# Gate rows through DRAM instead of TensorE transposes, in a two-block transformer kernel

## The reference, cut to what matters

```
mod = (silu_c @ w_mod[l] + b_mod[l]).reshape(B, 3 * N_SUB, 1, D)
x = macaron_half_ffn(x, norm_g[l, 0], *mod_terms(mod, 0), ffn_w_in[l, 0], ffn_w_out[l, 0])
# macaron_half_ffn: x + 0.5 * gate * swiglu(modulate(x, g, shift, scale), w_in, w_out)
sh, sc, gt = mod_terms(mod, 1)
h = modulate(x, norm_g[l, 1], sh, sc)
x = x + gt * y            # y: attention and mLSTM mixer in layer 0, spatial gating in layer 1
```

## Time and profile before

| | |
|---|---|
| median of 3 runs | 1588.73 us (1588.63 to 1588.76) |
| the profiled execution, first to last instruction (span) | 1587.4 us |
| what lies around the span, against the median | 1.3 us |
| PE / DVE / ACT / POOL busy | 1565.0 / 1173.0 / 777.5 / 70.5 us |
| transposes of gate columns, first and last start | 72, at 138.1 and 1520.7 us |
| DMA, mean over the span | 212 GB/s |

### The profile page before, as it was taken

The page is one execution under the profiler, slowest core; times in us unless marked ns, Lnnn a source line. Parts: engine busy times, 40 slices in busy tenths (PEclk is TensorE's granted clock), DMA queues, the critical chain, the costliest instruction groups (busy, mean ns, idle before and its releaser), DMA issues.

```text
span 1587.4 us, 20744 instructions
## 1 busy us (share of the span) xinstructions
PE 1565.0 (99%) x7994; PEld 1296.9 (82%) x7994; DVE 1173.0 (74%) x1917; ACT 777.5 (49%) x1246; POOL 70.5 (4%) x112
## 2 busy tenths in 40 slices
PE   7999999999999999999999999999999999999998
PEld 5887778888888888887777888888888888888887
DVE  7889899759886665477766888868877667666654
ACT  5767666532222222254556555445555463455552
POOL 2000000100000000030010100000000100010000
PEclk9999999999999999999999999999999999999999
DMA  9977676336656655252122777867777575455550
GB/s 376 373 290 273 234 251 224 107 127 231 213 212 239 224 212 179 87 175 80 67 95 72 281 302 292 311 219 264 255 280 274 210 308 187 171 203 187 186 190 30
DMA packets 93044, 336.97 MB, mean 212 GB/s; under 512 B 10625, under 2 KB 11265, under 8 KB 92690
## 3 DMA queue, kind: packets, MB, share of 16 engines
q1 hardware_dynamic: 90706, 327.58, 57.0%
q0 software_dynamic: 2240, 8.06, 1.5%
HBM read 334.56 MB, written 1.05 MB: 211 GB/s over the span
## 4 chain that ended last, share of the span: by engine, by line
PE 55%; DVE 2%; ACT 1%; issue 0%; POOL 0%; POOLq 0%; DVEq 0%; ACTq 0%
PE bank L292 53%; PE bank L295 2%; DVE sb_tm L301 0%; ACT sb_XN L298 0%; DVE sb_X L301 0%; ACT sb_arena L298 0%; ACT sb_XC L298 0%; DVE sb_arena L319 0%; DVE sb_arena L312 0%; DVE sb_XN L301 0%; DVE sb_sg L316 0%; DVE sb_XC L301 0%; DVE sb_w7r L301 0%; POOL sb_rstd L301 0%; DVE sb_w5r L301 0%
## 5 line engine op out<-in xcount | busy, mean ns | idle before, releaser
L292 PE MATMUL bank<-sb_hT,sb_hi 128*128 128x512 f32 (+1 forms) x1856 | 574.7, 379 | 0.0
L298 ACT ACTIVATE sb_hi<-sb_w 128x1024 fp32r<-128x1024 f32 x428 | 431.1, 1052 | 281.3 <-DMA sb_w<-in_w 238.1
L292 PEld LDWEIGHTS bank<-sb_hT,sb_hi 128*128 128x128 f32 x1856 | 332.1, 188 | 58.5 <-issue 0.2
L292 PE MATMUL bank<-sb_hi,sb_hT 128*128 128x512 f32 x1152 | 369.7, 395 | 2.9 <-ACT sb_hT L298 1.3
L292 PEld LDWEIGHTS bank<-sb_hi,sb_hT 128*128 128x128 f32 x1152 | 215.6, 188 | 53.2 <-issue 5.3
L312 DVE CUSTOM_DVE_ANT_0 sb_w<-sb_w,sb_cb 128x1024 f32<-128x1024 f32 x144 | 175.0, 1220 | 0.0
L301 DVE TENSOR_TENSOR sb_sg<-bank,sb_sg 128x512 f32<-128x512 f32 (+1 forms) x90 | 58.9, 660 | 101.5 <-ACT sb_sg L298 79.7
L298 ACT ACTIVATE sb_sg<-bank 128x512 f32<-128x512 f32 (+1 forms) x98 | 54.8, 573 | 118.0 <-PE bank L292 117.7
L298 ACT ACTIVATE sb_arena<-bank 128x512 f32<-128x512 f32 (+1 forms) x106 | 56.3, 558 | 55.9 <-PE bank L292 32.4
L301 DVE TENSOR_TENSOR sb_tm<-bank,sb_rows 128x512 f32<-128x512 f32 (+1 forms) x41 | 28.1, 684 | 69.5 <-PE bank L292 66.6
L298 ACT ACTIVATE sb_XN<-sb_X 128x512 f32<-128x512 f32 x33 | 20.7, 629 | 99.4 <-DVE sb_X L301 91.5
(11 more groups left out here) (483 smaller groups left out, 3211.4 us busy)
## 6 DMA issues: line engine op xcount, KB each, us to landing
sb_w<-in_w SPq DMA_DIRECT2D x428, 512.0 KB, 4.3
sb_w<-in_mw SPq DMA_DIRECT2D x192, 512.0 KB, 4.8
sb_rows<-in_na_rpb POOLq DMA_DIRECT2D x16, 96.0 KB, 2.9
sb_X<-in_x SPq DMA_DIRECT2D x1, 1024.0 KB, 4.9
sb_cb<-in_cvec POOLq DMA_DIRECT2D x2, 512.0 KB, 8.8
sb_XC<-in_ctx POOLq DMA_DIRECT2D x1, 1024.0 KB, 12.8
sb_arena<-in_sg_ln_g POOLq DMA_DIRECT2D x1, 1024.0 KB, 7.2
sb_arena<-in_sg_ln_b POOLq DMA_DIRECT2D x1, 1024.0 KB, 10.5
```

Of the source, the lines that this page charges most:

```text
L292: return self.e.matmul(out, a, b, start=start, stop=stop)
L298: return self.e.activation(out, a, f, **kw)
```

## The change

The gates no longer pass through PE and ACT. For each of the nine, POOL issues a DMA that writes the eight columns of `mods` to a row of 1024 numbers in DRAM (`gate_rows`, a new tensor), waits until that has landed, and issues a second DMA that reads the row back into all 128 partitions of `G`. DVE's first product with a gate waits for this load instead of ACT's copy. The core of the diff; the rest drops the calls in `pe_*` and `act_*` and renames the waits:

```diff
+    def dma_scattered(self, out, a):
+        return self.e.dma_start(out, a, allow_slow_non_contiguous=True)
...
-        def pe_gate(e, target, ring_):
-            e.wait_ge(*modulated(target))
-            for nh in range(2):
-                b = BANK["gate", target, nh] = ring_.take()
-                for f in b.free():
-                    e.wait_ge(*f)
-                for c4 in range(4):
-                    c = nh * 4 + c4
-                    m = e.tr(b.ap[:, c4 * 128:(c4 + 1) * 128], mods[:, TG[target], c:c + 1].to_broadcast([128, 128]), ident)
-                m.then_inc(GBC.sem, GBC.put(target, nh))
-                b.till = ((AE, "gate", target, nh),)
-
-        def act_gate(e, target, g, *after):
-            for nh in range(2):
-                e.wait_ge(*done(GBC, target, nh))
-                for s, *what in after:
-                    e.wait_ge(*done(s, *what))
-                e.act(g[:, nh * 512:(nh + 1) * 512], BANK["gate", target, nh].ap[:, :], ACT.Copy).then_inc(
-                    AE.sem, AE.put("gate", target, nh))
+        GROW = {"a0": 0, "a1": 1, "m00": 2, "x00": 0, "m01": 1, "m02": 2, "m10": 0, "m11": 1, "m12": 2}
+        gate_rows = nc.dram_tensor("gate_rows", (len(GROW), D), F32).ap()
+
+        def pool_gate(e, stage, *after):
+            row, load = gate_rows[list(GROW).index(stage)], LD[f"g{GROW[stage]}"]
+            e.wait_ge(*modulated(stage + "gt"))
+            e.dma_scattered(row.rearrange("(c p) -> p c", p=128), mods[:, TG[stage + "gt"], :]).then_inc(
+                LD["row"].sem, LD["row"].put(stage, by=16))
+            for s, *what in after:
+                e.wait_ge(*done(s, *what))
+            e.wait_ge(*done(LD["row"], stage))
+            e.dma(G[GROW[stage]][:, :], row.partition_broadcast(128)).then_inc(load.sem, load.put(stage, by=16))
...
             def gated(j, nh):
                 e.wait_ge(*done(SQ, p, j, nh))
-                e.wait_ge(*done(AE, "gate", f"a{l}gt", nh))
+                e.wait_ge(*gate_row(f"a{l}"))
...
         def pool_block1(e, l):
-            if l == 1:
+            if l == 0:
+                pool_gate(e, "a0")
+            else:
                 pool_rstd(e, "cx0")
                 pool_norm(e, "cx0")
+                pool_gate(e, "a1")
             s, _, p = edge(l)
...
+            pool_gate(e, "m01", (SMX, "na", 15))
             pool_edge(e, "m02")
...
             pool_block1(e, 1)
+            pool_gate(e, "m00", (MOD, "tile", 47))
+            pool_gate(e, "x00", (RES, 0, 1, 1))
             pool_edge(e, "m01")
             pool_mixer(e)
+            pool_gate(e, "m02", (RES, "m00", 6, 1, 1))
             pool_edge(e, "m10")
+            pool_gate(e, "m10", (SMX, "na", 15), (DE, "mf", 3))
             pool_edge(e, "m11")
             pool_spatial(e)
+            pool_gate(e, "m12", (RES, "m02", 0, 1, 1))
```

More of the change, by code:

```diff
@@ L465, in build @@
         LD = {k: signal("load_" + k) for k in ("cb", "cb2", "cst", "cst2", "vec", "x", "pos", "xc", "blk", "small", "mlm", "nb0", "nb1", "nb2", "nb3",
-                                                "sg", "fg", "out")}
+                                                "sg", "fg", "out", "row", "g0", "g1", "g2")}
         slot_load = [signal(f"slot{i}") for i in range(NSLOT + NARENA + NCTX + NXC)]
@@ L960, in build @@
                 {3: ("q", 0), 7: ("k", 0), 11: ("v", 0), 15: ("q", 1), 19: ("k", 1), 23: ("v", 1), 27: ("g", 0), 31: ("g", 1)}]
-        B1 = [{13: [("tq", 0)], 14: [("tk", 0)], 30: [("gated", 0), ("y", 0)], 33: [("gate", 0)]},
+        B1 = [{13: [("tq", 0)], 14: [("tk", 0)], 30: [("gated", 0), ("y", 0)]},
               {6: [("tq", 0)], 9: [("tk", 0)], 29: [("gated", 0), ("y", 0)],
                30: [("cxn", 0)], 31: [("cx", 0)], 32: [("gated", 1), ("y", 1), ("cx", 1)],
[1 row of a table removed]
[1 row of a table added]
         for v in range(6):
@@ L1040, in items @@
                                       lambda c2, k=k, i=i: ((AE, "t" + k, l, i, c2),))
-                    elif what == "gate":
-                        pe_gate(e, f"a{l}gt", HB3)
                     elif what == "cx":
@@ L1337, in act_block1 @@
                                 AE.sem, AE.put("y", l, i, q))
-                    elif what == "gate":
-                        act_gate(e, f"a{l}gt", G[l])
                     elif what == "cx":
@@ L1614, in build @@
         NEXT = {"m00": "m01", "m02": "m10", "m10": "m11", "m12": "fin"}
-        GROW = {"m00": 2, "x00": 0, "m02": 2, "m10": 0, "m12": 2, "m01": 1, "m11": 1}
         def up_tile(s, b0, s11, k):
@@ L1762, in pe_ffn @@
                         pe_first_hidden(e, s)
[L1763 to L1766, removed]
                 n = b1 - b0
@@ L1961, in dve_gated @@
             e.wait_ge(*end)
-            e.wait_ge(*done(AE, "gate", gate, nh))
+            e.wait_ge(*gate_row(gate))
             e.wait_ge(DE, DE.n)
@@ L2059, in act_ffn @@
                     act_hidden(e, s, s11)
[L2060 to L2063, removed]
                 for nh in range(2):
@@ L2071, in act_ffn @@
             act_edge(e, NEXT[s], tail, (s, 6 if ns == 2 else 0), (1,), rows_turned(s), hT_free(NEXT[s]))
-        def gate_row_free(s):
-            return {"m00": [(MOD, "tile", 47)], "m02": [(RES, "m00", 6, 1, 1)], "m10": [(SMX, "na", 15), (DE, "mf", 3)],
-                    "m12": [(RES, "m02", 0, 1, 1)]}[s]
         def hT_free(s):
@@ L2101, in dve_ffn @@
                     for x in range(ns):
-                        dve_residual(e, (X, XC)[x], (G[GROW[s]], G[0])[x], (s + "gt", "x00gt")[x],
+                        dve_residual(e, (X, XC)[x], (G[GROW[s]], G[0])[x], (s, "x00")[x],
                                      BANK[key][2 * x:2 * x + 2], [ended(*key, 2 * x + j) for j in range(2)], nh,
@@ L2108, in residual @@
             def residual(j, nh=1):
[L2109 removed]
+                dve_gated(e, G[GROW[s]], s, BANK[key][j], ended(*key, j), nh, j, till)
                 dve_total(e, X, nh, j, till, (s, b0))
@@ L2150, in dve_context_tail @@
             key = ("d", "m00", 6, 1)
-            dve_residual(e, XC, G[0], "x00gt", BANK[key][2:4], [ended(*key, 2 + j) for j in range(2)], 1,
+            dve_residual(e, XC, G[0], "x00", BANK[key][2:4], [ended(*key, 2 + j) for j in range(2)], 1,
                          ("dm", "m00", 6, 1, 1), ("ctx", 6))
@@ L2198, in build @@
         MX.setdefault(29, []).append(("y", 0))
-        MX[31] += [("gate", 0), ("y", 1)]
+        MX[31] += [("y", 1)]
         def turned(kind, half):
@@ L2269, in pe_mixer @@
                         pe_neighbours(e, i)
-                    elif what == "gate":
-                        pe_gate(e, "m01gt", HB3)
             for j in range(2):
@@ L2708, in act_mixer @@
                         act_neighbours(e, i)
-                    elif what == "gate":
-                        act_gate(e, "m01gt", G[1], (SMX, "na", 15))
                     elif what == "y":
@@ L2841, in residual @@
             def residual(j, nh):
-                dve_gated(e, G[1], "m01gt", BANK["mo", nh][j], ended("mo", nh, j), nh, j, ("dm", "mx", nh))
+                dve_gated(e, G[1], "m01", BANK["mo", nh][j], ended("mo", nh, j), nh, j, ("dm", "mx", nh))
                 dve_total(e, X, nh, j, ("dm", "mx", nh), ("mx",))
@@ L3026, in dve_spatial @@
                 if u == 39:
-                    dve_residual(e, X, G[1], "m11gt", BANK["so", 0], [ended("so", 0, j) for j in range(2)], 0,
+                    dve_residual(e, X, G[1], "m11", BANK["so", 0], [ended("so", 0, j) for j in range(2)], 0,
                                  ("dm", "sg", 0), ("sg",))
             def residual(j, nh=1):
-                dve_gated(e, G[1], "m11gt", BANK["so", 1][j], ended("so", 1, j), 1, j, ("dm", "sg", 1))
+                dve_gated(e, G[1], "m11", BANK["so", 1][j], ended("so", 1, j), 1, j, ("dm", "sg", 1))
                 dve_total(e, X, 1, j, ("dm", "sg", 1), ("sg",))
@@ L3046, in pool_spatial @@
                 e.tt(q[:, 7:8], q[:, 7:8], minus_half[:, 0:1], ALU.pow).then_inc(PO.sem, PO.put("ln", j))
+            pool_gate(e, "m11", (RES, "mx", 1, 1))
             pool_edge(e, "m12")
```

6 lines of the change are left out of this document (2 added, 4 removed), and 2 rows, old and new, of the table B1.

## The result

| | before | after |
|---|---|---|
| median | 1588.74 us, 4 runs (1588.63 to 1588.97) | 1609.32 us, 4 runs (1607.67 to 1610.06) |
| ratio | | 1.0128, 95% interval 1.0115 to 1.0140 |
| span of the profiled execution | 1587.4 us | 1607.4 us |

The change makes the kernel 20.6 us slower. The forecast was 1588.0 us, range 1584.8 to 1593.5, with a chance of 0.25 for slower. It was wrong.

What follows compares the result with a forecast made beforehand. PE, busy 99% of the span, was taken to bound the kernel. Transposes removed won 5.4 us and a stall behind a1 cost 4.7, so -0.7 from 1588.73 gave 1588.0 us, no change that can be told; range 1584.8 to 1593.5.

Steps and rivals of the forecast that it cites:

- The gain: PE time won by dropping the gate transposes: 0.88 us at each of six, 0.1 at m01, none at a0, a1; 5.4 us.
- the stall: At the boundary a1 to m00, PE idles for a late G[1]: 7.27 us late less 2.6 covered, 4.7 us.
- W: Time for a1's row write on POOL to be issued and land: 1.9 + 3.4 = 5.3 us.
- R: Time for the 512 KB broadcast read of a1's row from issue to landing: 4.1 us, taken from final_g.
- I take 3.4, somewhat under the middle: Part of W after the issue, set at 3.4 us between gw's 1.5 and positions' 6.8.
- gw: Existing DMA, 128 pieces of 512 bytes, landing in 2.1 us; the lower bound for W.
- positions: Existing DMA, 128 pieces of 8 bytes, 7.2 us in the crowded start; used in bounding W after issue.
- the slow rival: Scattered write at a1 lasts as long as ctx, W = 12.8, stall 12.2, time 1595.5 us; chance 0.25, alone or with clock.
- I cost these at nothing; POOL's idle time hides them: The other eight gates' writes and reads, issued well before use, were forecast to cost 0 us.
- 1.4% more: Added transfer bytes of all nine gates, 9 x 512 KB, counted within the zero-cost term.
- the third rival: PE's clock falls during the a1 to m00 wait, price 1.9 us, time 1589.9 us; chance 0.25.
- The fit: Skill page's 2.0 us plus bytes over 436 GB/s for POOL's DMAs: write 2.0, read 3.2, stall 0.5, time 1583.9.

Runs made afterwards that it cites:

- the reads alone: The changed kernel without its nine writes, the broadcast reads taking final_g instead: 1583.29 us, ratio 0.9965.
- 8 bytes apart: The changed kernel with the 1024 numbers written 8 bytes apart in DRAM, the read taking final_g: 1592.72 us, one run.
- 512 bytes: The changed kernel with each number written to a DRAM line of its own, 512 bytes apart, the read taking final_g: 1590.53 us, ratio 1.0011.
- SBUF: The changed kernel with the 1024 pieces sent to a spare SBUF tile instead of DRAM, the read taking final_g: 1591.52 us, ratio 1.0016.
- 32 bytes: The changed kernel with the 1024 numbers written 32 bytes apart in DRAM, the read taking final_g: 1590.85 us, one run.
- 64 bytes: The changed kernel with the 1024 numbers written 64 bytes apart in DRAM, the read taking final_g: 1590.27 us, ratio 1.0011.
- 128 pieces: The changed kernel with the row written channel-permuted, 128 pieces of 32 bytes instead of 1024 of 4: 1587.87 us, ratio 0.9991.
- eight whole pieces: Against the changed kernel, one PE transpose and ACT copy per gate, POOL writing 8 pieces of 512 bytes, some earlier: 1586.19 us; m01's transpose moved too: 1584.55 us.
- the writes alone: The kernel before, gates still by transposes, with the nine scattered writes added on POOL and no reads: 1607.70 us, ratio 1.0117.

## Why the prediction was wrong

**The gain was right.** Forecast 5.4; the kernel with the reads alone has it, 1588.9 to 1583.3. Where it is won and where not (a0, a1, m01) came out as the timelines had it, gate by gate.

**The form of the stall was right, its size was not.** The prediction has G[1] at 298.17 + W + R, 7.27 us late, of which 2.6 are covered, so a stall of W + R - 4.73. In seven kernels:

| kernel | W | R | W + R - 4.73 | PE's wait |
|---|---|---|---|---|
| changed | 10.2 | 6.0 | 11.5 | 11.53 |
| 8 bytes apart | 5.4 | 5.5 | 6.2 | 6.28 |
| 512 bytes | 3.2 | 7.5 | 6.0 | 6.05 |
| SBUF | 2.9 | 6.8 | 5.0 | 5.12 |
| 32 bytes | 4.3 | 4.8 | 4.4 | 4.44 |
| 64 bytes | 3.3 | 5.7 | 4.2 | 4.32 |
| 128 pieces | 2.0 | 5.3 | 2.6 | 2.65 |

The term that was mis-sized is W, 10.2 for 5.3, and with it R, 6.0 for 4.1. With the reads alone, issued at 297.96, R is 4.0, so I put the rest down to the weight tiles that a later read meets. "I take 3.4, somewhat under the middle" is the sentence that failed. It built W from issuing and count. The issue was 0.96, not 1.9, and the count alone makes W 3.2, less than I had; the 7 us on top come from single numbers lying side by side in DRAM, which neither gw nor positions could show, as both are reads. W came to lie between 9.2, the point from which the slow rival decides, and its 12.8; that rival, at 0.25, was the nearest, but for its own place alone it gave 1595.5.

**The step that failed outright** is "I cost these at nothing; POOL's idle time hides them". POOL's idle time hides the waiting of POOL. It doesn't hide what the write does to the other transfers: some 7 us in which hardly a weight tile moves. 12.5 of the 25.6 us lost come from there, and the prediction had no term, no bound and no rival for it. It went by bytes ("1.4% more") and by low parts "some microseconds ahead of PE in all these places". What counts first is how far ahead of ACT the tiles land, at each write: before, 0.7 to 3.1 us for those that land between 92 and 103, 0.0 to 0.2 for four between 893 and 900, and over 20 for those near 302. The first two are less than the 7 us of a hold-up, and there PE paid; at 302 it paid nothing for tiles. That lead is a warning and not a price: before, the tiles between 389 and 439 land 0.0 us ahead of ACT too, and the changed kernel lost nothing there behind two writes. I take it that PE pays only when ACT's or DVE's delay outlasts the work that PE still has in hand; how much that is at each place is not measured.

**The sum, with what was measured.** The stall is 6.8 us over the forecast, the clock 1.6, the hold-ups 12.5 and the gain 0.2 under it. That is 21.1 us of the 21.3 between 1588.0 and 1609.3.

**The clock** fell, as the third rival said, 0.25 in the text. It costs 1.6 us at the boundary (1.9 forecast). It fell at the stall of all seven kernels of the table, and the shift beyond the wait is 1.6 to 2.8 us; those with waits of 4.3 and 4.4 lost 1.9 and 2.8. So it belonged to the forecast of a 4.7 us stall itself. Behind 1.63 us, at 293.58, the granted clock stays at 1.00.

**The fit.** The Trainium skill (DMA: Bandwidth & Descriptors, Anatomy of one DMA) gives an estimate of 2.0 us for this write. The row says 10.2. The median from issue to landing is 3.0 us for eight whole pieces and 2.0 for 128, so the fit agrees with the last and with no write of single numbers. What the Trainium skill says against single elements on the same page (Rules for kernel authors) pointed the right way, though one transfer per number alone cost little: W is 3.2 where the numbers lie 512 bytes apart.

## What to carry to other kernels

A DMA's price is not its own time on an idle queue: ask what else moves on the DMA engines while it is under way, and how far ahead of use those transfers are at each place where it is issued. Don't scatter single numbers side by side into DRAM; turn the data first, even at the price of a transpose, and write whole pieces. And a result that is ready early is only early if its place in the issuing engine's order is.

## What the runs showed of the hardware

- 1024 pieces of 4 bytes from SBUF, where the write's packets are over 2.3 us behind the issue: 2.6 us from issue to landing into SBUF, 2.9 to 3.3 into DRAM 512 bytes apart, 9.2 to 10.6 into 4 KB in one piece; up to 15.4 at other places of the changed kernel. The closer the numbers lie, the longer it takes.
- What differs there is the time from the last packet to the landing, 0.4 us for SBUF and 7.3 in the changed kernel, at m02.
- In that time, between 904 and 912, reads on another queue fall to 24 to 34 GB/s. Two such writes back to back kept ACT waiting 13.8 us for one weight tile.
- The same read of 512 KB took 4.0 us issued at 298 and 4.8 to 7.5 issued at 300 to 303, when weight tiles move too.
- Behind the start, PE's clock fell to its lower level at waits of 2.24 us (at 102.08, in the kernel with the writes alone), 2.65, 3.05 and more, and not at 1.63 or at 1.70 (913.93, in the kernel with the writes alone).
